# A two-layer hybrid diffusion step on one core: a longer ring for modulation weights, attention output formed token by feature, and a new order of the gated-linear-attention pass

## The chip, the cores and the metric

One core of a Trainium2 chip (trn2) runs the whole program. The metric is device time in microseconds (us), the median of the runs; lower is better. Engines are named as in the profile: PE (TensorE: matmuls, and PEld for its weight loads), DVE (VectorE), ACT (ScalarE), POOL (GpSimd), SP (SyncE, which issues most of the DMAs here).

## The reference, cut to what matters

```python
def adaln_layer(x, cond, mod_w, mod_b, norm_g, w1, w2, mixer):
    sh1, sc1, gt1, sh2, sc2, gt2 = modulation(cond, mod_w, mod_b)   # silu(cond) @ mod_w + mod_b
    h = rms_norm(x, norm_g[0]) * (1 + sc1) + sh1
    mix, aux = mixer(h)
    x = x + gt1 * rms_norm(mix, norm_g[1])
    ...
# layer 0 mixer: z = h @ w_in (2304 columns), then a gated convolution beside windowed attention
    s_loc = einsum(q, k of the own 128-token block and both neighbours) * scale, masked to +-128
    s_ctx = einsum(q, 256 cached context keys) * scale
    p = sink_softmax(concatenate([s_loc, s_ctx], -1), sink_f)   # 8 query heads, 2 key/value heads, 64 wide
    o = p[own] @ v_own + p[ctx] @ v_ctx
    return concatenate([conv_out, o], -1) @ w_out
# layer 1 mixer: bidirectional gated linear attention (GLA), 4 heads of 128 x 256, forward and backward
```

1152 tokens (128 prompt, 1024 latent) of 1024 features are 9 tiles of 128 tokens. All is float32. Products with the big weight matrices run as three float32r products of a high and a low part (hi x hi, hi x lo, lo x hi); attention and GLA use plain float32 products, each of which the trace shows as two loads and two matmuls.

## The kernel before, in words

Every engine has one program, written out by hand, with semaphores between them; nothing is scheduled by a compiler. An engine runs its list in order and stops at a wait. Three stages matter here.

**First pass** (54 units). A unit `u` is one 128-column panel of `ab_w_in` times 384 tokens: 24 matmuls of 384 columns into bank `u % 4` (`unit`). ACT empties the bank (`unit_take`). Between units the remaining 80 chunks of the modulation matrix are worked off. A chunk `k` is 512 KB: SP loads it into `mod_p[k % MODS]` once PE has used chunk `k - MODS` (`late_mod` on SP), ACT rounds it into `mod_ph` (`late_hi`), DVE subtracts to get the low part in place, `mod_pl` (`late_lo`), and PE multiplies both with the condition (`late_mod` on PE, 4 matmuls of 512 columns). Each four chunks finish one group of rows `q`: ACT copies the 4 x 512 sums out of PSUM (`late_rows`), PE turns them with four small transposes (`late_turn`, recorded at line 1687, the line of the helper `turn`), DVE adds them (`late_add`). Which chunks belong to a unit is `mods_after`, and which groups `rows_after`. In the list of ACT the rounding for unit `u + 1` stands behind `unit_take(u)`, and `late_rows` behind that rounding. From unit 18 on (`CONV_UNIT`) DVE also works out the convolution (`conv`), and in units 8 to 20 the rotary embedding (`rope`).

**Attention** (72 steps, `attention_steps`). A step is one block `b` of 128 queries and one head. Two steps (`u` = 0 and 1, heads `j` and `j + 4`) are a pair, 36 pairs in all. Block 0 has 1 tile of 128 keys, blocks 1 and 8 have 4, blocks 2 to 7 have 5 (24 pairs). The loop is staggered: in iteration `it` PE forms the scores of step `it` (line 1838), turns the probabilities of step `it - 2` (line 1687) and multiplies those of step `it - 3` with v (line 1864). DVE adds the band mask (1383), takes the maximum (1386, 1388), and for the step before divides the probabilities by their sum (1370, 1371, 1373). ACT takes the exponential (832, 835) and copies the turned probabilities of step `it - 3` to `prT` (822), three tiles; DVE copies the others (1359). The product with v has v as the stationary operand (64 columns) and 128 columns of `prT` as the moving one, so that the two heads of a pair come out feature by token, one above the other, in bank 2; ACT and DVE split that into `at_hi` (827) and `at_lo` (1364).

**GLA, backward pass** (9 tiles, `TURNS`). For each tile there are seven levels of decayed products. POOL forms gaps of the decay sums (lines 628 to 639), ACT takes their exponentials into PSUM (`exp_factor`, 1077 to 1085), DVE scales q and k (`scale`, 1581), PE multiplies (`gram`, 2099), DVE puts the result under a mask into `att` (`place`, 1591). Between levels stand, for the tile before, the update of the state (`update` on PE, 2086, and `state_step` on DVE, 1603) and its output (`att_out` on PE, 16 matmuls of 256 columns, 2116 and 2118; `o_take` on ACT, 1101), and a turn of k (`turn_k`).

Of the kernel before, what the change touches and what calls it, by code (L numbers as in the profile page):

```python
# [25 lines left out]
P = 128  # L26
# [17 lines left out]
GH = 4  # L44
# [7 lines left out]
MODS = 3  # L52
# [38 lines left out]
def build(nc, io):  # L91
# [17 lines left out]
    mod_p = [at(f"mod_p{i}", [P, 2, 512], F32, RW + 6 * PANEL + 2 * PANEL * i) for i in range(MODS)]  # L109
    mod_pl = [at(f"mod_pl{i}", [P, 2, 512], F32R, RW + 6 * PANEL + 2 * PANEL * i) for i in range(MODS)]  # L110
    mod_ph = [at(f"mod_ph{i}", [P, 2, 512], F32R, RW + 7 * PANEL + 2 * PANEL * i) for i in range(MODS)]
# [32 lines left out]
    smx = at("smx", [P, 3, 8], F32, o + 34816)  # L144
# [82 lines left out]
    with ExitStack() as ctx:  # L227
# [67 lines left out]
        s_norm = sem("s_norm")  # L295
        pt_ready = sem("pt_ready")
        pt_a = sem("pt_a")
        pt_v = sem("pt_v")
# [59 lines left out]
        O_BANK = 2  # L358
# [6 lines left out]

        def mods_after(u):
# [297 lines left out]
        def _(act):  # L664
# [150 lines left out]
            for it in range(len(steps) + 4):  # L815
                if 3 <= it < len(steps) + 3:
                    b, j, u, tiles = steps[it - 3]
# [6 lines left out]
                if it >= 4 and steps[it - 4][2] == 1:  # L824
                    b, j, u, tiles = steps[it - 4]
                    act.wait_ge(pv_ready, it - 3)
                    nc.scalar.activation(at_hi[:, b, j, :], ps[:, O_BANK, 0:P], ACT.Copy).then_inc(ao_hi, 1)
                if it < len(steps):
                    b, j, u, tiles = steps[it]
                    x = smx[:, it % 3, :]  # L830
                    act.wait_ge(s_max, it + 1)
                    nc.scalar.activation(prob[it % 3][:, 0:len(tiles) * P], s_bank(it)[:, 0:len(tiles) * P], ACT.Exp,  # L832
                                         bias=x[:, 1:2], accum_out=x[:, 2:3])
                    head = j + 4 * u
                    nc.scalar.activation(x[:, 3:4], sink[:, head:head + 1], ACT.Exp, bias=x[:, 1:2]).then_inc(s_exp, 1)
# [267 lines left out]
            for a, tile in enumerate(TURNS):  # L1103
                if tile != 1:
                    exp_factor("k1", tile)
                for level in range(NL):
                    if LEVELS[level] > 1:
                        exp_factor("S", tile, level)
                    if level == 0:
# [5 lines left out]
                    exp_factor("M", tile, level)  # L1115
# [5 lines left out]
                    if level == 4 and a:  # L1121
# [63 lines left out]
        def _(dve):  # L1185
# [85 lines left out]
            def late_lo(k):  # L1271

                dve.wait_ge(mod_hi, FIRST_LO + k + 1)
                V.tensor_tensor(mod_pl[k % MODS][:], mod_p[k % MODS][:], mod_ph[k % MODS][:].bitcast(F32),  # L1274
# [75 lines left out]
            wide = 0  # L1350
            for it in range(len(steps) + 4):
                if 3 <= it < len(steps) + 3:
                    b, j, u, tiles = steps[it - 3]
                    if len(tiles) > 3:
                        dve.wait_ge(pt_ready, it - 2)
                        if it >= 5:
                            dve.wait_ge(pv_ready, it - 4)
                        m = len(tiles) - 3
                        V.tensor_copy(prT[(it - 3) % 2][:, 3:3 + m, :],
                                      ps[:, 1, 0:m * P].rearrange("p (t n) -> p t n", t=m)).then_inc(pt_v, 1)  # L1360
                if it >= 4 and steps[it - 4][2] == 1:
                    b, j, u, tiles = steps[it - 4]
                    dve.wait_ge(ao_hi, (it - 4) // 2 + 1)
                    V.tensor_tensor(at_lo[:, b, j, :], ps[:, O_BANK, 0:P], at_hi[:, b, j, :].bitcast(F32),
                                    ALU.subtract).then_inc(ao_lo, 1)
                if 1 <= it <= len(steps):
                    b, j, u, tiles = steps[it - 1]
                    x = smx[:, (it - 1) % 3, :]
                    dve.wait_ge(s_exp, it)
                    own(V.tensor_tensor(x[:, 4:5], x[:, 2:3], x[:, 3:4], ALU.add))  # L1370
                    own(V.reciprocal(x[:, 5:6], x[:, 4:5]))
                    pr = prob[(it - 1) % 3][:, 0:len(tiles) * P]
                    V.tensor_scalar(pr, pr, x[:, 5:6], None, ALU.mult).then_inc(s_norm, 1)  # L1373
                if it < len(steps):
                    b, j, u, tiles = steps[it]
                    x = smx[:, it % 3, :]
# [9 lines left out]
                    own(V.tensor_reduce(x[:, 0:1], s[:, 0:len(tiles) * P], AX_X, ALU.max))  # L1386
# [850 lines left out]
```

## Time and profile before

| | before |
|---|---|
| median of 3 runs | 3229.49 us (3227.47 to 3234.83) |
| profiled execution, its time | 3222.65 us |
| span of its instructions | 3220.9 us |
| PE busy (matmul) | 2972.4 us, 92% |
| DVE busy | 1636.6 us, 51% |
| ACT busy | 1340.6 us, 42% |
| POOL busy | 159.7 us, 5% |

The three stages above lie at about 65 to 462, 463 to 731 and 2009 to 2222 us of the span. The rest is the opening, the output projections, two MLPs, the GLA projection and the forward pass; PE is busy there nearly all the time.

### The profile page before, as it was taken

The numbers are of one execution on the slowest core, as the hardware profiler recorded it, in microseconds if no ns is written. First come the engines' busy times: TensorE is split into PE (matmuls) and PEld (weight loads), VectorE is DVE, ScalarE is ACT, GpSimd is POOL, SyncE is SP. The second block draws the span as 40 slices with busy tenths as digits, with TensorE's granted clock in tenths as the row PEclk, the third lists the DMA queues.
The fourth block names the chain that finished last, engine by engine and source line by source line (L and its number), as shares of the span: only waits on it lengthen the run. The fifth ranks groups of instructions, "written<-read, shape, count | busy, mean of one in ns | idle before, by whom it ended". The sixth has DMA issues, their size and how long they took to land.

```text
span 3220.9 us, 39879 instructions
## 1 busy us (share of the span) xinstructions
PE 2972.4 (92%) x14994; PEld 2575.5 (80%) x14994; DVE 1636.6 (51%) x2527; ACT 1340.6 (42%) x2151; POOL 159.7 (5%) x260
## 2 busy tenths in 40 slices
PE   6888888888999999999999999777799999999998
PEld 3667676667899999999989877666679999999997
DVE  6444546664645454454442254766554545445444
ACT  6333333334544344344332366554444344334333
POOL 0000000000000000000000000873000000000000
PEclk8989989999999999999999999878899999999999
DMA  5444420005334443443331343001434444444443
GB/s 218 131 136 143 140 85 1 1 1 150 111 119 124 124 147 121 130 144 125 124 106 46 107 136 124 13 1 60 151 110 124 125 124 144 127 127 144 128 126 111
DMA packets 309592, 355.15 MB, mean 110 GB/s; under 512 B 20070, under 2 KB 242604, under 8 KB 308428
## 3 DMA queue, kind: packets, MB, share of 16 engines
q1 hardware_dynamic: 300560, 331.52, 32.9%
q10 hardware_dynamic: 6876, 13.87, 1.2%
q0 software_dynamic: 2016, 7.86, 0.7%
q8 instruction: 91, 1.49, 0.2%
q14 instruction: 49, 0.40, 0.0%
HBM read 337.88 MB, written 15.34 MB: 110 GB/s over the span
## 4 chain that ended last, share of the span: by engine, by line
PE 78%; DVE 9%; ACT 6%; issue 4%; DMA 3%; ACTq 0%; DVEq 0%; SPq 0%
PE ps L1897 35%; PE ps L1956 24%; PE ps L1746 7%; PE ps L2012 4%; PE ps L2099 2%; DMA mod_p<-mod_w 2%; PE ps L1687 2%; DVE smx L1386 1%; PE ps L1764 1%; DVE prob L1373 1%; DVE t_g L1409 1%; ACT junk_n L848 1%; DVE ps L1383 1%; PE ps L2116 1%; ACT mod_ph L726 0%
## 5 line engine op out<-in xcount | busy, mean ns | idle before, releaser
L1213 DVE TENSOR_TENSOR p_lo<-p_raw,p_hi 128x1024 fp32r<-128x1024 f32 x507 | 619.6, 1224 | 682.8 <-ACT p_hi L708 682.6
L708 ACT ACTIVATE p_hi<-p_raw 128x1024 fp32r<-128x1024 f32 x507 | 532.8, 1052 | 543.0 <-DMA p_raw<-mlp_w 398.7
L1956 PE MATMUL ps<-hm_hi,p_hi 128*128 128x384 f32 x1536 | 517.3, 337 | 4.8 <-DVE hm_lo L1233 4.0
L1956 PE MATMUL ps<-hm_hi,p_lo 128*128 128x384 f32 x1536 | 517.1, 337 | 0.0
L1956 PE MATMUL ps<-hm_lo,p_hi 128*128 128x384 f32 x1536 | 516.0, 336 | 0.0
L1897 PE MATMUL ps<-p_hi,hid_hi 128*128 128x512 f32 x1152 | 362.6, 396 | 1.9 <-DVE p_lo L1213 1.9
L1897 PE MATMUL ps<-p_lo,hid_hi 128*128 128x512 f32 x1152 | 357.3, 391 | 0.0
L1897 PE MATMUL ps<-p_hi,hid_lo 128*128 128x512 f32 x1152 | 356.5, 391 | 0.0
L893 ACT ACTIVATE relu<-ps 128x384 f32<-128x384 f32 x192 | 94.4, 492 | 547.9 <-PE ps L1956 547.9
L1447 DVE TENSOR_TENSOR sqr<-relu 128x384 f32<-128x384 f32 x192 | 107.2, 558 | 396.3 <-ACT relu L893 396.3
L1956 PEld LDWEIGHTS ps<-hm_hi,p_hi 128*128 128x128 f32 x1536 | 289.4, 188 | 14.1 <-DVE hm_lo L1233 4.5
L1956 PEld LDWEIGHTS ps<-hm_lo,p_hi 128*128 128x128 f32 x1536 | 289.5, 188 | 7.2
L1956 PEld LDWEIGHTS ps<-hm_hi,p_lo 128*128 128x128 f32 x1536 | 289.4, 188 | 0.0
L1897 PEld LDWEIGHTS ps<-p_lo,hid_hi 128*128 128x128 f32 x1152 | 216.3, 188 | 48.1
L1897 PEld LDWEIGHTS ps<-p_hi,hid_lo 128*128 128x128 f32 x1152 | 216.2, 188 | 47.6
L1897 PEld LDWEIGHTS ps<-p_hi,hid_hi 128*128 128x128 f32 x1152 | 210.3, 188 | 34.3 <-DVE p_lo L1213 2.4
L1274 DVE TENSOR_TENSOR mod_pl<-mod_p,mod_ph 128x1024 fp32r<-128x1024 f32 x80 | 96.9, 1224 | 180.5 <-ACT mod_ph L726 180.4
L1746 PE MATMUL ps<-h_hi,p_hi 128*128 128x384 f32 x432 | 159.5, 369 | 0.0
L1746 PE MATMUL ps<-h_lo,p_hi 128*128 128x384 f32 x432 | 151.3, 350 | 0.0
L1746 PE MATMUL ps<-h_hi,p_lo 128*128 128x384 f32 x432 | 151.2, 350 | 0.0
L2099 PE MATMUL ps<-xx,xx 128*128 128x128 f32 x432 | 76.1, 342 | 56.0 <-DVE xx L1581 34.5
L832 ACT ACTIVATE prob<-ps,smx 128x640 f32<-128x640 f32 (+2 forms) x72 | 52.0, 722 | 160.4 <-DVE smx L1388 160.4
(238 smaller groups left out, 4344.4 us busy)
## 6 DMA issues: line engine op xcount, KB each, us to landing
p_raw<-mlp_w SPq DMA_DIRECT2D x384, 512.0 KB, 3.8
mod_p<-mod_w SPq DMA_DIRECT2D x80, 512.0 KB, 4.1
p_raw<-gla_w_in SPq DMA_DIRECT2D x56, 512.0 KB, 3.6
p_raw<-gla_w_out SPq DMA_DIRECT2D x24, 512.0 KB, 3.4
mod_w<-mod_w SPq DMA_DIRECT2D x8, 1024.0 KB, 13.4
p_raw<-ab_w_in SPq DMA_DIRECT2D x14, 512.0 KB, 5.5
p_raw<-ab_w_out SPq DMA_DIRECT2D x12, 512.0 KB, 3.5
p_raw<-ab_w_out SPq DMA_DIRECT2D x24, 256.0 KB, 3.8
```

The lines of the kernel that those rows point to most:

```text
L708: nc.scalar.activation(p_hi[s][:, :, 0:width], p_raw[s][:, :, 0:width], ACT.Copy).then_inc(pan_hi, 1)
L832: nc.scalar.activation(prob[it % 3][:, 0:len(tiles) * P], s_bank(it)[:, 0:len(tiles) * P], ACT.Exp, bias=x[:, 1:2], accum_out=x[:, 2:3])
L893: nc.scalar.activation(relu[b][:], ps[:, b, 0:GN], ACT.Relu).then_inc(up_read[b], 1)
L1213: V.tensor_tensor(p_lo[s][:, :, 0:width], p_raw[s][:, :, 0:width], p_hi[s][:, :, 0:width].bitcast(F32), ALU.subtract).then_inc(pan_lo, 1)
L1274: V.tensor_tensor(mod_pl[k % MODS][:], mod_p[k % MODS][:], mod_ph[k % MODS][:].bitcast(F32), ALU.subtract).then_inc(mod_lo, 1)
L1447: V.tensor_tensor(sqr[b][:], relu[b][:], relu[b][:], ALU.mult).then_inc(sq_ready, 1)
L1687: return M.transpose(out, in_, ident[0:n, 0:n])
L1746: mm = M.matmul(ps[:, b, 0:GN], w[s][:, c, :], h0[n][x][:, c, :], start=(c == 0 and x == 0 and w is p_hi), stop=(c == DC - 1 and w is p_lo))
L1897: mm = M.matmul(acc(t)[:, cols], x, flat(w[s])[:, cols], start=begin and edge == 0, stop=end and edge == 2)
L1956: mm = M.matmul(ps[:, b, 0:GN], w[s][:, c, :], x[:, c, :], start=(c == 0 and x is hi and w is p_hi), stop=(c == DC - 1 and w is p_lo))
L2012: mm = M.matmul(ps[0:width, b, 0:GN], w[s][:, c, 0:width], hx[g][x][:, c, :], start=(c == 0 and x == 0 and w is p_hi), stop=(c == DC - 1 a ...
L2099: last = M.matmul(ps[:, i % 2, h * P:(h + 1) * P], stationary[:, h, :], moving[:, h, :], start=True, stop=True)
```

## The change

1. First pass: `MODS` goes from 3 to 4 raw buffers, and the rounded parts get a ring of their own of `MOD_HI` = 2 (the same six panels of memory). Chunks are given out two to a unit from unit 2 on, fewer in some units of the convolution. `late_rows` goes ahead of `unit_take` in ACT's list.
2. Attention: the probabilities are turned unscaled. The product with v now has the turned probabilities as the stationary operand (128 columns) and 64 columns of v as the moving one, so that the output stands token by feature, both heads of a pair side by side. DVE scales it with the reciprocal sums when it takes it from PSUM (two instructions of 64 columns, into `at_n`), PE turns it once for both heads into bank 7 (`AT_BANK`), and from there it is split. ACT alone copies `prT`, now 640 columns. Sum and reciprocal are formed once a pair.
3. GLA, backward: ACT's exponential for `M` goes ahead of the copy to `att` at level 0; `att_out` goes in two halves, behind the products of levels 2 and 3; `o_take` and `state_step` move from level 4 to 5, `turn_k` from level 5 to 6.

```diff
-MODS = 3
+MODS = 4
+MOD_HI = 2
...
+        mod_unit = []
+        for u in range(2, 49):
+            conv_u0 = u - CONV_UNIT
+            few = conv_u0 >= 0 and conv_u0 % 9 in (0, 4, 7)
+            mod_unit += [] if conv_u0 % 9 == 7 and few else [u] if few else [u, u]
+        mod_unit = mod_unit[:LATE]
...
-            return [k for k in range(LATE) if 2 + 46 * k // LATE == u]
+            return [k for k in range(LATE) if mod_unit[k] == u]
...
-            return [q for q in range(LATE // 4) if 2 + 46 * (4 * q + 3) // LATE + 1 == u]
+            return [q for q in range(LATE // 4) if mod_unit[4 * q + 3] + 1 == u]
...
-                if k >= MODS:
-                    act.wait_ge(modp_used, FIRST_USED + k - MODS + 1)
-                nc.scalar.activation(mod_ph[k % MODS][:], mod_p[k % MODS][:], ACT.Copy).then_inc(mod_hi, 1)
+                if k >= MOD_HI:
+                    act.wait_ge(modp_used, FIRST_USED + k - MOD_HI + 1)
+                nc.scalar.activation(mod_ph[k % MOD_HI][:], mod_p[k % MODS][:], ACT.Copy).then_inc(mod_hi, 1)
...
+                for q in rows_after(u):
+                    late_rows(q)
                 unit_take(u)
                 for k in mods_after(u + 1):
                     late_hi(k)
-                for q in rows_after(u):
-                    late_rows(q)
...
-                    m = min(3, len(tiles))
-                    nc.scalar.activation(prT[(it - 3) % 2][:, 0:m, :], ps[:, 0, 0:m * P].rearrange("p (t n) -> p t n", t=m),
+                    nc.scalar.activation(prT[(it - 3) % 2][:].rearrange("p t n -> p (t n)")[:, 0:n], psf[:, 0:n],
                                          ACT.Copy).then_inc(pt_a, 1)
...
+                if it >= 7 and it % 2:
+                    b, j, u, tiles = steps[it - 7]
+                    act.wait_ge(at_turned, (it - 7) // 2 + 1)
+                    nc.scalar.activation(at_hi[:, b, j, :], ps[:, AT_BANK, 0:P], ACT.Copy).then_inc(ao_hi, 1)
...
-                    V.tensor_scalar(pr, pr, x[:, 5:6], None, ALU.mult).then_inc(s_norm, 1)
...
+                    dve.wait_ge(pv_ready, 2 * pair + 2)
+                    if pair >= 2:
+                        dve.wait_ge(at_turned, pair - 1)
+                    for u in range(2):
+                        last = V.tensor_scalar(at_n[pair % 2][:, u, :], ps[:, O_BANK, HD * u:HD * (u + 1)], r[:, u:u + 1], None,
+                                               ALU.mult)
+                    last.then_inc(at_norm, 1)
...
+                if it >= 8 and it % 2 == 0:
+                    b, j, u, tiles = steps[it - 8]
+                    dve.wait_ge(ao_hi, (it - 8) // 2 + 1)
+                    V.tensor_tensor(at_lo[:, b, j, :], ps[:, AT_BANK, 0:P], at_hi[:, b, j, :].bitcast(F32),
+                                    ALU.subtract).then_inc(ao_lo, 1)
...
-                    pe.wait_ge(s_norm, it - 1)
+                    pe.wait_ge(s_exp, it - 1)
...
+                if it >= 6 and it % 2 == 0:
+                    pair = (it - 6) // 2
+                    pe.wait_ge(at_norm, pair + 1)
+                    if pair:
+                        pe.wait_ge(ao_lo, pair)
+                    turn(ps[:, AT_BANK, 0:P], at_n[pair % 2][:].rearrange("p u d -> p (u d)")).then_inc(at_turned, 1)
...
-                        last = M.matmul(ps[cols, O_BANK, 0:P], v, prT[(it - 3) % 2][:, pos, :],
+                        last = M.matmul(ps[:, O_BANK, cols], prT[(it - 3) % 2][:, pos, :], v,
                                         start=(pos == 0), stop=(pos == len(tiles) - 1))
...
+                    exp_factor("M", tile, level)
                     if level == 0:
...
-                    exp_factor("M", tile, level)
...
-                    if level == 4 and a:
+                    if level == 5 and a:
                         o_take(a - 1)
...
-                    if level == 4 and a:
+                    if level == 5 and a:
                         dve.wait_ge(ob_ready, a)
...
                     if level == 1 and a:
                         update(a - 1, TURNS[a - 1])
-                        att_out(a - 1)
-                    if level == 5 and tile != 1:
+                    if level in (2, 3) and a:
+                        att_out(a - 1, 2 * (level - 2), 2 * (level - 1))
+                    if level == 6 and tile != 1:
```

How the instructions stand on an engine, at three places. ACT in the first pass, units 13 and 14 of the kernel before (`mod_r` is the copy of `late_rows`, `q_t` that of `unit_take`, `mod_ph` that of `late_hi`):

```order
L744 ACTIVATE q_t<-ps 128x384 [waits unit_done3]
L726 ACTIVATE mod_ph_77<-mod_p_71 128x1024 [waits modp_used,modp_landed0]
L726 ACTIVATE mod_ph_78<-mod_p_72 128x1024 [waits modp_used,modp_landed1]
L733 ACTIVATE mod_r<-ps 4x512 [waits mod_turned,modp_used]
L708 ACTIVATE p_hi_171<-p_raw_163 128x1024 [waits pan_in2]
```

and of the changed kernel:

```order
L743 ACTIVATE mod_r<-ps 4x512 [waits mod_turned,modp_used]
L754 ACTIVATE q_t<-ps 128x384 [waits unit_done2]
L736 ACTIVATE mod_ph_79<-mod_p_73 128x1024 [waits modp_used,modp_landed2]
L736 ACTIVATE mod_ph_80<-mod_p_74 128x1024 [waits modp_used,modp_landed3]
L754 ACTIVATE q_t<-ps 128x384 [waits unit_done3]
```

The copy of the sums stood behind two roundings, each of which waits for a landing; it now stands ahead of the unit's own copy and of the roundings that belong to it.

DVE in the attention of blocks 2 to 7, one pair, before:

```order
L1383 TENSOR_TENSOR ps<-ps,band 128x128 [waits s_ready]
L1386 TENSOR_REDUCE smx<-ps 128x1 [waits dve_own]
L1388 TENSOR_SCALAR smx<-smx,sink 128x1 [waits dve_own]
L1359 COPY prT_106<-ps 128x256 [waits pv_ready,pt_ready]
L1364 TENSOR_TENSOR at_lo<-ps,at_hi 128x128 [waits ao_hi]
L1370 TENSOR_TENSOR smx<-smx 128x1 [waits s_exp]
L1371 RECIPROCAL smx<-smx 128x1 [waits dve_own]
L1373 TENSOR_SCALAR prob_104<-prob_104,smx 128x640 [waits dve_own]
```

and now (first an odd iteration, then an even one):

```order
L1368 TENSOR_SCALAR at_n_110<-ps,smx 128x64 [waits at_turned,pv_ready]
L1380 TENSOR_TENSOR ps<-ps,band 128x128 [waits s_ready]
L1383 TENSOR_REDUCE smx<-ps 128x1 [waits dve_own]
L1385 TENSOR_SCALAR smx<-smx,sink 128x1 [waits dve_own]
L1390 TENSOR_TENSOR smx<-smx 128x2 [waits s_exp]
L1391 RECIPROCAL smx<-smx 128x2 [waits dve_own]
L1380 TENSOR_TENSOR ps<-ps,band 128x128 [waits s_ready,dve_own]
L1395 TENSOR_TENSOR at_lo<-ps,at_hi 128x128 [waits ao_hi]
```

The 640-column scaling and the copy to `prT` are gone from DVE; `at_lo` stands behind the maximum of its iteration.

PE in the same stage, the even iteration of the changed kernel, in which the output of a pair is turned:

```order
L1844 MATMUL ps<-kc_t,q_t 128x256 [waits s_exp]
L1844 MATMUL ps<-k_t,q_t 128x256
L1844 MATMUL ps<-k_t,q_t 128x128
L1694 MATMUL ps<-ident,prob_106 128x128 [waits pt_a,s_exp]
L1694 MATMUL ps<-ident,at_n_110 128x128 [waits ao_lo,at_norm]
L1869 MATMUL ps<-v_c,prT_108 128x64 [waits pt_a]
```

The turn of `at_n` waits for `ao_lo`, the count of `at_lo`, which DVE raises in the same even iteration, behind the maximum of the scores that head this list.

## Rows read from the trace of the kernel before

**Rows 1.** Windows: busy us and instructions of each engine, TensorE clock, DMA share, GB/s.

```profile
core 0: us, PE busy (x) PEld busy (x) DVE busy (x) ACT busy (x) POOL busy (x), PEclk, DMA share, GB/s
82.00:461.50 379.50, 328.27 (x1656) 266.24 (x1654) 174.57 (x230) 127.48 (x172) 0.00 (x0) 0.94 0.42 132
479.20:507.90 28.70, 27.82 (x106) 18.20 (x105) 16.71 (x58) 10.54 (x36) 0.00 (x0) 0.65 0.00 1
507.90:698.40 190.50, 159.77 (x1001) 129.57 (x1000) 131.62 (x409) 73.34 (x216) 0.00 (x0) 0.97 0.00 1
2010.00:2222.00 212.00, 155.10 (x812) 142.82 (x810) 145.44 (x241) 106.72 (x178) 152.08 (x245) 0.79 0.03 10
```

**Rows 2.** Waits, first pass (65 to 462 us): us in total, times, longest.

```profile
ACT mod_ph L726 <- DMA mod_p<-mod_w: 74.4, 25, 3.6
PE ps L1687 <- ACT mod_r L733: 42.0, 14, 4.7
PE ps L1687 <- ACT v_n L799: 4.7, 1, 4.7
```

**Rows 3.** The chain that ended last, first pass: start, us, what.

```profile
93.88 1.07 ACT mod_ph L726
94.97 1.24 DVE mod_pl L1274
...
297.96 1.85 PE ps L1764 x8
...
440.52 21.04 PE ps L1746 x120
```

**Rows 4.** DMA issues of the stage: count, KB each, median us to landing.

```profile
mod_p<-mod_w SPq DMA_DIRECT2D x71, 512.0 KB, 4.0
```

**Rows 5.** Timeline, one `late_turn`, weight loads: start, us, engine, instruction.

```profile
97.27 0.32 PEld L1687 LDWEIGHTS ps<-ident,mod_r 4*128 4x128 f32 x4 [0.47 <-ACT mod_r L733]
```

**Rows 6.** Timeline, attention, one pair of five-tile steps.

```profile
602.27 0.49 DVE L1383 TENSOR_TENSOR ps<-ps,band 128x128 f32<-128x128 f32 x2
...
603.01 0.70 PE L1838 MATMUL ps<-kc_t,q_t 64*128 64x256 f32 x2
...
603.54 0.81 PE L1838 MATMUL ps<-k_t,q_t 64*128 64x256 f32 x4
603.65 0.22 DVE L1388 TENSOR_SCALAR smx<-smx,sink 128x1 f32<-128x1 f32 x1
603.78 0.41 DVE L1359 COPY prT<-ps 128x256 f32<-128x256 f32 x1
603.90 0.79 ACT L832 ACTIVATE prob<-ps,smx 128x640 f32<-128x640 f32 x1 [2.73 <-DVE smx L1388]
...
604.87 0.48 ACT L822 ACTIVATE prT<-ps 128x384 f32<-128x384 f32 x1
...
609.04 0.74 PE L1687 MATMUL ps<-ident,prob 128*128 128x128 f32 x5 [0.34 <-issue]
609.14 0.29 DVE L1364 TENSOR_TENSOR at_lo<-ps,at_hi 128x128 fp32r<-128x128 f32 x1 [1.35 <-ACT at_hi L827]
...
609.71 0.41 PEld L1864 LDWEIGHTS ps<-prT,v_c 128*64 128x64 f32 x4 [0.17 <-issue]
...
610.94 0.29 PEld L1838 LDWEIGHTS ps<-kc_t,q_t 64*128 64x128 f32 x2 [0.17 <-issue]
```

**Rows 7.** Timeline, attention, block 1: scores and turn of four tiles, no wait between.

```profile
499.07 0.74 PE L1838 MATMUL ps<-kc_t,q_t 64*128 64x256 f32 x2
...
500.18 0.66 PE L1687 MATMUL ps<-ident,prob 128*128 128x128 f32 x4
```

**Rows 8.** Timeline, GLA, one tile of the backward pass.

```profile
2108.43 1.95 PE L2099 MATMUL ps<-xx,xx 128*128 128x128 f32 x16
...
2109.53 0.74 DVE L1591 COPY_PREDICATED att<-masks,ps 128x512 f32<-128x512 int32 x1 [2.88 <-PE ps L2099]
...
2122.23 0.69 DVE L1581 TENSOR_TENSOR xx<-gq,ps 128x512 f32<-128x512 f32 x1 [1.81 <-ACT ps L1085]
```

More of the change, by code:

```diff
@@ L108, in build @@
     mod_r4 = at("mod_r4", [4, 2 * D], F32, RS + 1024)
-    mod_p = [at(f"mod_p{i}", [P, 2, 512], F32, RW + 6 * PANEL + 2 * PANEL * i) for i in range(MODS)]
-    mod_pl = [at(f"mod_pl{i}", [P, 2, 512], F32R, RW + 6 * PANEL + 2 * PANEL * i) for i in range(MODS)]
-    mod_ph = [at(f"mod_ph{i}", [P, 2, 512], F32R, RW + 7 * PANEL + 2 * PANEL * i) for i in range(MODS)]
+    mod_p = [at(f"mod_p{i}", [P, 2, 512], F32, RW + (6 + i) * PANEL) for i in range(MODS)]
+    mod_pl = [at(f"mod_pl{i}", [P, 2, 512], F32R, RW + (6 + i) * PANEL) for i in range(MODS)]
+    mod_ph = [at(f"mod_ph{i}", [P, 2, 512], F32R, RW + (6 + MODS + i) * PANEL) for i in range(MOD_HI)]
     def acts(name, dt, r, chunks=DC):
@@ L143, in build @@
     prT = [at(f"prT{i}", [P, 5, P], F32, o + 29696 + 2560 * i) for i in range(2)]
-    smx = at("smx", [P, 3, 8], F32, o + 34816)
+    smx = at("smx", [P, 3, 4, 2], F32, o + 34816)
+    at_n = [at(f"at_n{i}", [P, 2, HD], F32, o + 34944 + 512 * i) for i in range(2)]
     gq = at("gq", [P, TILES, GH, P], F32, RD)
@@ L814, in _ @@
             steps = attention_steps()
-            for it in range(len(steps) + 4):
+            for it in range(len(steps) + 7):
                 if 3 <= it < len(steps) + 3:
-                    b, j, u, tiles = steps[it - 3]
+                    n = len(steps[it - 3][3]) * P
                     act.wait_ge(pt_ready, it - 2)
@@ L1349, in _ @@
             steps = attention_steps()
[L1350 to L1372, printed above, removed]
-                    V.tensor_scalar(pr, pr, x[:, 5:6], None, ALU.mult).then_inc(s_norm, 1)
+            for it in range(len(steps) + 8):
+                pair = (it - 5) // 2
+                if it >= 5 and it % 2 and pair < len(steps) // 2:
+                    r = smx[:, pair % 3, 0]
+                    dve.wait_ge(pv_ready, 2 * pair + 2)
[5 more added lines that the diff above has]
+                    last.then_inc(at_norm, 1)
                 if it < len(steps):
                     b, j, u, tiles = steps[it]
-                    x = smx[:, it % 3, :]
+                    x = smx[:, it // 2 % 3]
                     s = s_bank(it)
@@ L1385, in _ @@
                         own(last)
-                    own(V.tensor_reduce(x[:, 0:1], s[:, 0:len(tiles) * P], AX_X, ALU.max))
+                    own(V.tensor_reduce(x[:, 0, u:u + 1], s[:, 0:len(tiles) * P], AX_X, ALU.max))
                     head = j + 4 * u
-                    V.tensor_scalar(x[:, 1:2], x[:, 0:1], sink[:, head:head + 1], -1.0, ALU.max, ALU.mult).then_inc(s_max, 1)
+                    V.tensor_scalar(x[:, 1, u:u + 1], x[:, 0, u:u + 1], sink[:, head:head + 1], -1.0, ALU.max,
+                                    ALU.mult).then_inc(s_max, 1)
+                if it >= 3 and it % 2 and it - 2 < len(steps):
+                    x = smx[:, (it - 3) // 2 % 3]
+                    dve.wait_ge(s_exp, it - 1)
+                    own(V.tensor_tensor(x[:, 2], x[:, 2], x[:, 3], ALU.add))
+                    own(V.reciprocal(x[:, 0], x[:, 2]))
+                if it >= 8 and it % 2 == 0:
[3 more added lines that the diff above has]
+                                    ALU.subtract).then_inc(ao_lo, 1)
             dve.wait_ge(mods_ready, 2)
@@ L1761, in late_mod @@
                 pe.wait_ge(mod_lo, FIRST_LO + k + 1)
-                for w in (mod_ph[k % MODS], mod_pl[k % MODS]):
+                for w in (mod_ph[k % MOD_HI], mod_pl[k % MODS]):
                     for a in range(2):
                         last = M.matmul(ps[0:4, 4 + q % 2, :], csr[:, 2 * (k % 4) + a, :], w[:, a, :],
-                                        start=(k % 4 == 0 and a == 0 and w is mod_ph[k % MODS]),
+                                        start=(k % 4 == 0 and a == 0 and w is mod_ph[k % MOD_HI]),
                                         stop=(k % 4 == 3 and a == 1 and w is mod_pl[k % MODS]))
@@ L1820, in _ @@
             steps = attention_steps()
-            wide = [i for i, st_ in enumerate(steps) if len(st_[3]) > 3]
-            for it in range(len(steps) + 3):
+            for it in range(len(steps) + 5):
                 if it < len(steps):
@@ L2100, in gram, with att_out @@
                 last.then_inc(gram_ready, 1)
-            def att_out(a):
+            def att_out(a, h0, h1):
                 tile = TURNS[a]
-                pe.wait_ge(gram_taken, NL * (a + 1))
-                if a:
-                    pe.wait_ge(ob_taken, a)
-                    pe.wait_ge(xt_ready, factor_at[("q1", tile, 0)] + 1)
-                pe.wait_ge(khn_ready, min(a + 1, TILES - 1))
-                if a == 1:
-                    pe.wait_ge(st_in, 16)
-                if a >= 2:
-                    pe.wait_ge(st_ready, a)
-                for h in range(GH):
+                if h0 == 0:
+                    pe.wait_ge(gram_taken, NL * (a + 1))
+                    if a:
+                        pe.wait_ge(ob_taken, a)
+                        pe.wait_ge(xt_ready, factor_at[("q1", tile, 0)] + 1)
+                    pe.wait_ge(khn_ready, min(a + 1, TILES - 1))
+                    if a == 1:
+                        pe.wait_ge(st_in, 16)
+                    if a >= 2:
+                        pe.wait_ge(st_ready, a)
+                for h in range(h0, h1):
                     o = psf[:, 3 * 512 + DV * h:3 * 512 + DV * (h + 1)]
@@ L2134, in _ @@
                         turn_k(kh, 3)
-            att_out(TILES - 1)
+            att_out(TILES - 1, 0, GH)
             def turn_k0(tile):
```

36 lines of the change are left out of this document (14 added, 22 removed).

## The prediction

> **What bounds the kernel now.** I read the windows first, for how full PE is in the three stages that change, then in each stage the waits and the timeline, because the stages have different limits.
>
> In the first pass PE is busy 328.3 of 379.5 us and its granted clock is 0.94 on the mean [rows 1]. So 51.2 us are idle, and up to 0.06 x 379.5 = 22.8 us are lost to stretches at the lower of its two levels (1.2 against 2.4 GHz). The reader is to see in the waits where the idle time lies: 42.0 us of it stand before the four small transposes of `late_turn`, which wait for ACT's copy `mod_r` [rows 2]. ACT itself is not full (127 of 379.5 us [rows 1]). It stands for 74.4 us before the rounding of chunks that have not landed [rows 2], and the copy is queued behind these roundings. Ring and order together make the wait; no engine is the bound.
>
> In the attention of blocks 2 to 7 (190.5 us for 24 pairs, 7.94 us each) PE is busy 84% and DVE 69% [rows 1], and neither is full. One step runs through DVE (mask, maximum), ACT (exponential), DVE (sum, reciprocal, scaling) before DVE may begin the next mask, so the two take turns. The timeline shows ACT idle 2.73 us for the maximum, and DVE idle 1.35 us for `at_hi` [rows 6].
>
> In the backward pass of GLA (212 us for 9 tiles, 23.6 each) the clock is down to 0.79, and PE 73%, DVE 69%, POOL 72% are all half waiting [rows 1]. Twice per tile DVE stands for something that only the order puts ahead: 2.88 us for a product that is behind the 16 matmuls of `att_out`, and 1.81 us for an exponential that is behind ACT's copy to `att` [rows 8].
>
> **The change, part by part.**
>
> *First pass.* The work is the same: 54 units, 80 chunks. A unit takes PE 21.04 / 5 = 4.21 us, a chunk 1.85 / 2 = 0.93 [rows 3], so a unit with two chunks lasts 6.06 us. A buffer freed by chunk k of one unit is needed again for rounding behind the unit copy of the next, at least 0.93 + 4.21 = 5.1 us later; a landing takes 4.0 [rows 4]. The load is two chunks a unit and a panel in three units, 3.5 MB in 18.2 us or 192 GB/s; now 132 GB/s take a DMA share of 0.42 [rows 1], so that would take 0.61. Two roundings and two subtractions (1.07 and 1.24 each [rows 3]) behind a unit's end are done about 0.5 + 0.93 + 2.1 + 1.24 = 4.8 us later, ahead of the 6.06 at which PE wants them; the second ring of two holds them. That is the cover: with landings of 6 us or more it is gone, and `late_hi` waits again. The copy `mod_r` now needs only what PE did a unit ago, so the 42.0 us go. I leave 8 us of idle time: the wait for `v_n` (4.7 [rows 2], its place is unchanged and now meets two roundings) and about 1 us at each of three places where the long convolution on DVE comes ahead of a subtraction. Of the clock loss I count back 16 of 22.8, since full PE stretches (the five units of [rows 3]) run at the higher level. Saved: 51.2 - 8 + 16 = 59 us. Bounds: 74 (all), and 25 if the wait only moves to the landing.
>
> *Attention.* DVE loses the scaling, the copy and half the sums; it no longer waits for the exponential of the step before. ACT's copy grows from 384 to 640 columns (0.48 us to about 0.7); its 0.97 us from exponential to copy stays [rows 6], so 1.7 us a step, far from full. What comes last now? PE's list. An even iteration begins with the scores: issued at 0, drained at 0.53 + 0.81 = 1.34. DVE then needs 1.51 from the first mask to the instruction behind the maximum, and 0.29 for `at_lo` [rows 6]. With 0.03 and 0.10 from engine to engine (0.03 is seen from maximum to exponential, 0.10 is my estimate), the turn of `at_n`, which waits for this `at_lo`, starts at 3.27. Scores and turn of the five tiles would be through at 1.35 + 0.67 = 2.02 (1.11 in [rows 7] for four tiles, and 2 x 0.122 for the fifth; 609.04 to 609.71 in [rows 6]). So a new wait of 1.25 us per pair takes the place of DVE's. Behind it on PE stand the product with v and the next scores, and all of DVE and ACT follows these. Turn and switch are 0.22 (one fifth of 0.67, and some 0.09). If V is the product with v, an even iteration is 3.49 + V, an odd one 2.02 + V, a pair 5.51 + 2V.
>
> V is the unknown. Now 64 stationary and 128 moving columns take 1.23 us (609.71 to 610.94, of which 0.17 is issue [rows 6]). Afterwards it is 128 stationary and 64 moving. No row has this. The nearest is the GLA product with 128 of both: 16 in 1.95, 0.122 each [rows 8]. That is more than the 1.06 / 10 = 0.106 with 64 stationary columns, so there the load sets the pace, and halving what moves should not help. Below: 4 loads of 128 columns for transposes, with 4 moving, take 0.32 [rows 5], 0.08 each at most, but those are one pass, not two. V is 10 x 0.122 + 0.15 = 1.37 by the first, 0.95 by the second. I take the first: same kind of instruction. A pair is then 8.25, 0.31 more than now, x 24 = +7 us. Pairs of four tiles wait in the same way; block 1 runs mostly at the lower clock (0.65 [rows 1]), where PE's part counts double: +3. The longer tail (scaling, turn, split): +1. Together +11; from V = 0.95: 24 x -0.53 = -13, with the other two terms -9.
>
> The Trainium skill, on the page TensorE: Matmul & The Clock Gate, section LDWEIGHTS (loading the stationary operand), speaks against this edit: the time of a weight load goes with the columns of the stationary operand, not with its depth, and the change doubles them. By its figure, 128 / 1.2 = 107 ns, V would be 1.22 and a pair 7.95, attention +4 and the kernel 3148. The trace does not have the figure: its one-pass load is at most 80 ns, its two-pass spacing 122.
>
> *GLA.* If both order waits vanish, 2.88 + 1.81 = 4.7 us a tile. The product of level 2 is no longer behind 16 matmuls, and half of `att_out` falls into PE's waits. Given back: `turn_k` behind the last level makes DVE's next `kh` wait, about 0.6; POOL, busy 152.1 / 9 = 16.9 us a tile [rows 1], becomes nearly full at 19, which costs some 0.7. I take 3.4 x 8 tiles (the first has no tile before it) = 27. Bounds: 0, if another wait ends at the same time, and (23.6 - 16.9) x 8 = 54, where POOL is the bound.
>
> **Sum:** -59 + 11 - 27 = -75. The profiled execution took 3222.65, so 3147.7; the median of the runs is 6.8 above it, so 3154.5, given as 3155.
>
> **The rivals.**
> 1. *The product with v follows its moving columns*: 0.061 each, V = 0.76, pair 7.03, -22, with the rest about -22: 3229.5 - 59 - 27 - 25 = 3118. For it: PE hides loads behind matmuls elsewhere. Against it: 0.122 with 128 stationary columns [rows 8]. 0.14.
> 2. *The ring is still short*: landings at 192 GB/s take over 6 us and PE waits for `mod_pl` in place of `mod_r`. First pass -25: 3189. The share of 0.61 speaks against it, a panel ahead in the queue for it. 0.12.
> 3. *The GLA order does not do what it says*: POOL or the low clock (0.79) keeps the period, 0 in place of -27: 3182. 0.10.
> 4. *Slower*: the granted clock. In attention PE now waits 1.25 us in one piece each pair. If it ran blocks 2 to 7 at the lower level, the even iteration is 2.44 + 0.03 + 1.80 + 0.10 + 0.35 + 2.6 = 7.3, the odd 2.45 + 1.3 + 2.6 = 6.35, a pair 13.7, so +138: 3229.5 - 86 + 142 = 3285. It decides from 86 / 5.8 = 15 of 24 pairs on. Against it: the clock is 0.97 today with waits as long [rows 1, 6]; for it: 0.65 in block 1. 0.04.
>
> **How the numbers follow.** Forecast 0.60, the rivals 0.14, 0.12, 0.10, 0.04. The likeliest gives 3155; its own range is 3132 to 3178 (first pass 45 to 68, GLA 15 to 38, attention 0 to 20, not all at one end). The range for 8 in 10 reaches into rivals 1, 2 and 3: 3122 to 3188. A measurement of this kernel tells 0.2% (6.5 us) from no change. Faster 0.94 (all but rival 4 and mixtures), same 0.02, slower 0.04.
>
> **What would show it.** First pass: the waits have no `mod_r` of tens of us, DMA waits of ACT fall below 20 us, the stage (first chunk's product to last unit) lasts about 320 us at a clock near 0.98. Attention: a row of PE waiting for DVE `at_lo` before a line 1694 transpose, about 36 x 1.2 = 43 us; a pair lasts 8.1 to 8.4 us; ten loads of `prT` take 1.2 us. GLA: a tile lasts near 20 us, and PE's gap before the level 2 product is gone. The prediction fails if V is below 1 us, if PE's waits for `mod_pl` reach 20 us, or if the clock rows of attention fall below 0.9.

## The result, and the profile after

The changed kernel takes 3266.55 us (median of 4 runs, 3265.22 to 3271.31) against 3229.52 us of the kernel before (4 runs on the same chip). Its ratio to before is 1.0115, with a 95% interval of 1.0097 to 1.0132. It is 37 us slower; I had forecast 75 us faster, and the time lies far outside the range. It lies 18 us below the 3285 us of the slower rival.

Three stages changed, and they went different ways. The page of the changed kernel, span and granted clock in 40 slices of 81.6 us each:

```profile
span 3265.5 us, 39825 instructions
PE   5999999999999999999999999877799999999998
PEclk8999955555999999999999999988999999999999
```

The five slices with a 5 are the attention. The reader should see that the row above them does not fall with them: PE is listed as busy while its clock is granted at the lower of its two levels, 1.2 GHz. The windows of the changed kernel say the same with numbers:

```profile
core 0: us, PE busy (x) PEld busy (x) DVE busy (x) ACT busy (x) POOL busy (x), PEclk, DMA share, GB/s
82.00:395.20 313.20, 307.89 (x1656) 250.06 (x1655) 171.90 (x230) 129.02 (x172) 0.00 (x0) 1.00 0.50 158
397.00:409.30 12.30, 9.16 (x34) 6.75 (x34) 6.29 (x34) 6.86 (x30) 0.00 (x0) 0.63 0.30 97
409.30:440.00 30.70, 27.33 (x85) 19.40 (x85) 11.48 (x38) 9.68 (x32) 0.00 (x0) 0.50 0.00 1
440.00:760.00 320.00, 299.92 (x1084) 253.55 (x1085) 100.80 (x330) 88.63 (x233) 0.00 (x0) 0.50 0.00 1
803.00:850.00 47.00, 41.87 (x178) 33.49 (x179) 20.18 (x20) 20.16 (x30) 0.00 (x0) 0.93 0.60 190
...
2080.00:2241.00 161.00, 121.99 (x720) 110.90 (x720) 130.12 (x214) 94.66 (x161) 141.63 (x230) 0.87 0.04 15
```

**First pass.** The stretch that took 379.5 us [rows 1] takes 313.2, with 5.3 us idle and the upper level throughout: 66.3 us saved.

**Attention.** The exponentials of the 72 steps show its length, first to last start, for the kernel before and then for the changed one:

```profile
L832 ACT ACTIVATE prob<-ps,smx x72: 367/793/794, 465.7 to 727.3; 128x640 f32<-128x640 f32 x48, 128x512 f32<-128x512 f32 x16, 128x128 f32<-128x128 f32 x8
```

```profile
L841 ACT ACTIVATE prob<-ps,smx x72: 354/793/795, 399.3 to 791.5; 128x640 f32<-128x640 f32 x48, 128x512 f32<-128x512 f32 x16, 128x128 f32<-128x128 f32 x8
```

That is 392.2 us instead of 261.6, 130.6 more. With its end (the last output is turned and split; the last `at_lo` is done at 733.4 us before and at 802.3 now) it is 403.0 instead of 267.7, 135.3 more. The lower level begins in block 0 and stays for the whole stage. The timeline of one pair of five-tile steps, PE, from the even step's scores (597.15) to those of the next pair (609.83):

```profile
597.15 1.22 PE L1844 MATMUL ps<-kc_t,q_t 64*128 64x256 f32 x2
598.17 1.49 PE L1844 MATMUL ps<-k_t,q_t 64*128 64x256 f32 x4
...
601.71 0.45 PE L1694 MATMUL ps<-ident,at_n 128*128 128x128 f32 x1 [0.80 <-DVE at_lo L1395]
...
604.11 1.22 PE L1844 MATMUL ps<-kc_t,q_t 64*128 64x256 f32 x2
...
606.54 1.33 PE L1694 MATMUL ps<-ident,prob 128*128 128x128 f32 x5
607.67 0.96 PE L1869 MATMUL ps<-v_c,prT 128*128 128x64 f32 x4
608.42 1.49 PE L1869 MATMUL ps<-v_n,prT 128*128 128x64 f32 x6
609.83 1.22 PE L1844 MATMUL ps<-kc_t,q_t 64*128 64x256 f32 x2
```

A pair takes 12.68 us (6.96 even, 5.72 odd) in place of 7.94. The two score rows that headed a pair before, 0.70 and 0.81 [rows 6], are 1.22 and 1.49 now, and the product with v takes 609.83 - 607.67 = 2.16. The waits of the stage (397 to 803 us) have the row that I had forecast, PE for `at_lo`; I had put it at 43 us, and it is 26.4:

```profile
ACT prob L841 <- DVE smx L1385: 279.9, 70, 5.1
DVE ps L1380 <- PE ps L1844: 175.4, 64, 3.9
DVE at_n L1368 <- PE ps L1869: 86.8, 35, 4.0
...
PE ps L1694 <- DVE at_lo L1395: 26.4, 33, 1.3
```

DVE waits for PE and ACT for DVE, while PE is idle for 31 of the 406 us. PE is the bound of this stage now.

**GLA, backward.** From the first to the last product of level 0 it is 158.9 us (2080.8 to 2239.7) instead of 183.2: 24.3 saved. DVE's wait ahead of `att` fell from 31.9 to 10.9 us:

```profile
DVE att L1598 <- PE ps L2104: 10.9, 17, 1.2
```

The sum of the stages is -66.3 - 24.3 + 135.3 = +44.7, and the spans differ by 3265.5 - 3220.9 = 44.6 (the medians by 37; the profiled execution of before, 3222.65 us, lies 6.9 below its median). So the whole result is in three known places. Two gained about what they should. What has to be explained is why the clock stayed down.

### The profile page after: what moved, and what is told of

The parts are those of the page before. It is cut to its first block and busy times, and to the rows that moved or that the text cites. A ratio compares the mean times of both kernels' runs of the same rounds, so it can differ in the third digit from the quotient of the medians.

```text
span 3265.5 us, 39825 instructions
## 1 busy us (share of the span) xinstructions
PE 3087.6 (95%) x15030; PEld 2680.1 (82%) x15030; DVE 1587.0 (49%) x2391; ACT 1352.7 (41%) x2151; POOL 159.2 (5%) x260
## 3 DMA queue, kind: packets, MB, share of 16 engines
q8 instruction: 91, 1.49, 0.2%
## 5 line engine op out<-in xcount | busy, mean ns | idle before, releaser
L1753 PE MATMUL ps<-h_hi,p_hi 128*128 128x384 f32 x432 | 151.8, 351 | 0.0
L1457 DVE TENSOR_TENSOR hid_lo<-sqr,hid_hi 128x384 fp32r<-128x384 f32 x192 | 107.3, 559 | 18.5 <-DVE sqr L1454 0.4
```

Of the source, the lines that this page charges most:

```text
L1457: V.tensor_tensor(hid[layer][b][1][:], sqr[b][:], hid[layer][b][0][:].bitcast(F32), ALU.subtract).then_inc(hid_lo, 1)
L1753: mm = M.matmul(ps[:, b, 0:GN], w[s][:, c, :], h0[n][x][:, c, :], start=(c == 0 and x == 0 and w is p_hi), stop=(c == DC - 1 and w is p_lo))
```

## The experiments

The theories, before the runs. A: the product with v in its new form (a load of 128 columns ahead of each 64 moving ones) keeps the clock low, however busy PE is listed. B: PE's wait for `at_lo`, once a pair, keeps it low. C: the level depends on how block 0 is entered, and stays from there. D: the fuller first pass ahead of it is needed. C was put up after the first four runs of the stage (`e1_old_attention`, `e2_attention_alone`, `e3_both_heads_of_v`, `e5_lo_first`), the others before them. The table lists the experiments in their order below; "exponentials" is the time from the first to the last start of the 72. The kernel before, run on the same chips, gave 3228.57 us (beside e1, e2, e3 and e5), 3230.24 (e4, e6, e7, e8) and 3228.09 (e9, e10). Where a row has one run, it has no interval; the other kernels' runs spread over 3 to 19 us, so of these rows only differences well above that, or readings of the stage itself, are used.

| run | us (runs) | ratio to before | clock of the span | exponentials, us |
|---|---|---|---|---|
| e1_old_attention | 3131.7 (4) | 0.9698 (0.9681 to 0.9714) | 0.975 | 260.1 |
| e2_attention_alone | 3363.78 (1) | | 0.91 | 392.2 |
| e3_both_heads_of_v | 3150.2 (4) | 0.9771 (0.9741 to 0.9801) | 0.972 | 271.2 |
| e5_lo_first | 3240.89 (1) | | 0.923 | 358.7 |
| e4_filled_block0 | 3272.04 (1) | | 0.925 | 389.8 |
| e8_filled_lo_first | 3245.22 (1) | | 0.927 | 366.9 |
| e6_wide_lo_first | 3097.43 (4) | 0.9593 (0.9577 to 0.9609) | 0.976 | 219.3 |
| e7_rows_behind | 3180.21 (1) | | 0.969 | 261.9 |
| e9_ring_of_three | 3154.3 (4) | 0.9771 (0.9755 to 0.9787) | 0.971 | 261.8 |
| e10_gla_before | 3156.19 (4) | 0.9783 (0.9766 to 0.9799) | 0.972 | 260.4 |

### The attention of before in the changed kernel, and the new attention alone

`e1_old_attention` takes the three attention loops, their semaphores and tiles from the kernel before and leaves the first pass and GLA changed. `e2_attention_alone` is the reverse.

```diff
-    smx = at("smx", [P, 3, 4, 2], F32, o + 34816)
-    at_n = [at(f"at_n{i}", [P, 2, HD], F32, o + 34944 + 512 * i) for i in range(2)]
+    smx = at("smx", [P, 3, 8], F32, o + 34816)
...
-                        last = M.matmul(ps[:, O_BANK, cols], prT[(it - 3) % 2][:, pos, :], v,
+                        last = M.matmul(ps[cols, O_BANK, 0:P], v, prT[(it - 3) % 2][:, pos, :],
```

> The changed kernel with the attention of the kernel before; first pass and GLA stay as changed. Theory A (the low clock comes with the new attention itself): the granted clock recovers some 34 us into attention as before, attention takes 268 to 272 us, the kernel about 3229.5 - 66.5 - 24.4 = 3139 us. Rival D (it comes from the fuller first pass ahead of it): the clock stays at the lower level here too, attention takes well over 320 us, and the kernel is above 3190.

> The kernel before with the new attention alone. Theory A: the clock stays at the lower level for the whole of attention as in the changed kernel, which costs 135 us: about 3356 to 3360 us. Rival D (the fuller first pass is needed for it): the clock recovers, attention takes 270 to 285 us, the kernel 3230 to 3245.

Without the new attention the other two parts give 3131.7 us, 97 less than before; with it alone the kernel is 135 us slower (one run). Both met theory A; they came out 7 us below the 3139 and 4 above the 3360 that it gave. The window of `e1_old_attention` in which the changed kernel has 0.50:

```profile
440.00:600.00 160.00, 132.22 (x842) 107.03 (x841) 110.90 (x345) 61.27 (x181) 0.00 (x0) 0.99 0.00 1
```

PE is busy for 83% of it at the upper level. In `e2_attention_alone` the exponentials take 392.2 us, to the tenth what they take in the changed kernel, behind the first pass of before. Its clock is down there too:

```profile
480.00:800.00 320.00, 297.86 (x1061) 248.28 (x1061) 102.62 (x336) 89.66 (x241) 0.00 (x0) 0.50 0.00 1
```

D falls: the attention makes its own clock.

### Both heads of v as the moving operand

Only the moving operand of the product with v is widened from one head's 64 columns to all 128. The half that belongs to the other head is worked out and not read. Everything else, the wait for `at_lo` too, stays.

```diff
-                        v = v_c[:, tile, cols] if what == "ctx" else v_n[:, tile, cols]
-                        last = M.matmul(ps[:, O_BANK, cols], prT[(it - 3) % 2][:, pos, :], v,
+                        v = v_c[:, tile, :] if what == "ctx" else v_n[:, tile, :]
+                        last = M.matmul(ps[:, O_BANK, P * u:P * (u + 1)], prT[(it - 3) % 2][:, pos, :], v,
```

> The changed kernel, but the product with v moves all 128 columns of v (both key/value heads; the half that isn't wanted is left unread) past the same 128 stationary columns, so that loads, waits and order stay and only the moving columns of this product double. Theory A1 (the clock stays low because PE streams too little between loads): the clock recovers within some 34 us, a pair takes about 8.3 us, attention 275 to 285 us, the kernel 3140 to 3150. Rival B (it is PE's wait for at_lo in each pair) and rival D: no recovery, a pair takes 11.2 us or more, the kernel about 3267.

More work for PE makes the kernel 116 us faster than the changed one. Windows of this kernel:

```profile
409.30:440.00 30.70, 26.48 (x111) 18.80 (x110) 13.57 (x47) 11.15 (x37) 0.00 (x0) 0.71 0.00 1
440.00:600.00 160.00, 135.16 (x797) 114.86 (x798) 74.18 (x244) 65.71 (x171) 0.00 (x0) 0.90 0.00 1
```

PE is less busy (84%) than in the changed kernel (94%), and its clock is 0.90 instead of 0.50. The wait for `at_lo` is still there, so it alone does not hold the clock down. Its timeline also gives the terms of my sum at the upper level. Scores of the even step begin at 563.01, of the odd one at 567.76, of the next pair at 570.85:

```profile
563.01 0.70 PE L1844 MATMUL ps<-kc_t,q_t 64*128 64x256 f32 x2
...
564.75 0.74 PE L1694 MATMUL ps<-ident,prob 128*128 128x128 f32 x5 [0.39 <-ACT prT L831]
...
566.41 0.30 PE L1694 MATMUL ps<-ident,at_n 128*128 128x128 f32 x1 [0.93 <-DVE at_lo L1395]
...
566.55 0.61 PE L1869 MATMUL ps<-v_c,prT 128*128 128x128 f32 x4
...
567.00 0.83 PE L1869 MATMUL ps<-v_n,prT 128*128 128x128 f32 x6
...
567.76 0.70 PE L1844 MATMUL ps<-kc_t,q_t 64*128 64x256 f32 x2
```

The turn of `at_n` starts 3.40 us behind the scores, the product takes 567.76 - 566.55 = 1.21, and a pair 7.84.

### The split ahead of the maximum

In DVE's even iteration `at_lo` goes ahead of mask and maximum, so that PE finds it done.

```diff
+                if it >= 8 and it % 2 == 0:
+                    b, j, u, tiles = steps[it - 8]
+                    dve.wait_ge(ao_hi, (it - 8) // 2 + 1)
+                    V.tensor_tensor(at_lo[:, b, j, :], ps[:, AT_BANK, 0:P], at_hi[:, b, j, :].bitcast(F32),
+                                    ALU.subtract).then_inc(ao_lo, 1)
                 if it < len(steps):
                     b, j, u, tiles = steps[it]
...
-                if it >= 8 and it % 2 == 0:
-                    b, j, u, tiles = steps[it - 8]
...
```

> The changed kernel with at_lo ahead of the maximum in DVE's even iteration, so that PE's turn of the output finds it done; nothing else is changed. Rival B (the wait for at_lo keeps the clock low): the clock recovers and the kernel takes 3130 to 3140. Theory A1: the 26 us of waits go, the clock stays at the lower level, attention shortens by 25 to 30 us, the kernel about 3238.

The window of this kernel is the clearest row of the study:

```profile
440.00:700.00 260.00, 260.00 (x961) 227.96 (x960) 91.82 (x295) 77.92 (x202) 0.00 (x0) 0.50 0.00 1
```

PE is listed as busy for 260.00 of 260.00 us, and the clock is at the lower level for all of it. The wait is gone, but the clock is not back. B falls. The exponentials take 33.5 us less than in the changed kernel, 7 more than the 26.4 us of listed waits. The whole kernel gains only 25.7, because later stages give some of it back; the same GLA stretch takes 162.7 us here and 158.9 there. That the kernel's gain equals the listed waits is chance.

### Block 0 filled up

Four products of 256 columns into a bank that nobody reads are added to each of the first nine iterations, so that the clock is up when block 1 begins. `e8_filled_lo_first` has both this and the edit above.

```diff
+                if it < 9:
+                    for _ in range(4):
+                        M.matmul(ps[:, 6, 0:256], ident[:], q_t[:, 0, 0:256], start=True, stop=True)
```

> The changed kernel with four extra products of 256 columns per iteration on PE through the nine iterations 0 to 8 of attention (block 0), into a bank that nothing reads, so that PE is full there and the clock should not fall at its start. If the low state holds only because attention begins in it (theory C), the clock stays at its upper level in blocks 1 to 8, a pair takes about 8.0 to 8.3 us, attention about 275 to 290 us and the kernel 3140 to 3155. If the narrow product itself can't hold the level (rival A2), the clock falls in one of the first dips and stays down: attention between 330 and 410 us, the kernel 3200 to 3275.

> Block 0 filled as in the run of that name, and at_lo ahead of the maximum, with the narrow product of the changed kernel. Theory C: the clock stays up and a pair loses the wait of about 1 us, the kernel 3115 to 3130. Rival A2: the clock falls and stays down, 3190 to 3250, less than the changed kernel by 25 us for the waits.

The windows of `e4_filled_block0`, block 0 and the first pairs of block 1:

```profile
410.00:420.00 10.00, 10.00 (x50) 8.18 (x49) 3.65 (x17) 2.92 (x13) 0.00 (x0) 1.00 0.01 2
420.00:430.00 10.00, 8.42 (x48) 6.19 (x47) 6.06 (x22) 5.48 (x18) 0.00 (x0) 1.00 0.00 0
430.00:450.00 20.00, 17.25 (x79) 13.84 (x79) 7.89 (x26) 7.75 (x23) 0.00 (x0) 0.69 0.00 1
450.00:500.00 50.00, 46.80 (x171) 39.59 (x170) 15.91 (x52) 13.92 (x37) 0.00 (x0) 0.50 0.00 0
```

The stage is entered at the upper level, holds it while the filling products run (the last is issued at about 420 us) and for some 16 us behind them, then falls and stays down. With the wait gone too (`e8_filled_lo_first`) it also stays down, with 366.9 us of exponentials:

```profile
450.00:700.00 250.00, 250.00 (x922) 219.06 (x922) 87.58 (x279) 75.53 (x197) 0.00 (x0) 0.50 0.00 1
```

C falls, and A is left: with the narrow product, and without filling, the stage neither reached the upper level nor kept it. One thing stays open. While the filling products ran, the narrow product was in the same list (two matmuls a step in block 0) and the level was the upper one. So these runs do not tell whether the product with v has to be the wider one, or whether more moved columns anywhere in the list would do; no run adds them elsewhere in blocks 1 to 8. The one stretch at the upper level also prices the narrow product, here for four tiles:

```profile
427.33 0.56 PE L1872 MATMUL ps<-v_c,prT 128*128 128x64 f32 x4
427.72 0.61 PE L1872 MATMUL ps<-v_n,prT 128*128 128x64 f32 x4
428.26 0.48 PE L1844 MATMUL ps<-kc_t,q_t 64*128 64x256 f32 x1
```

428.26 - 427.33 = 0.93 for eight, 0.116 each. The wide one takes 1.21 / 10 = 0.121. Half the moving columns save almost nothing. What the two have alike is the load of 128 columns, so I read it as what sets the pace.

### The two edits that help, together

> The wide product with v (128 moving columns) and at_lo ahead of the maximum, both. The clock recovers as with the wide product alone, and the wait for at_lo, 0.93 us in a pair at the upper level, goes: 30 us by the row of waits less what the next wait takes (ACT's copy of prT). Expected 3118 to 3132 us, below the kernel with the old attention (3131.7). If ACT's exponential and copy take the whole place of it, 3145 to 3150.

Its windows, and a pair of its timeline (517.92 to 524.65, 6.73 us):

```profile
409.30:440.00 30.70, 29.64 (x140) 22.61 (x140) 16.95 (x55) 13.99 (x45) 0.00 (x0) 0.77 0.00 1
440.00:600.00 160.00, 150.83 (x1023) 132.30 (x1022) 96.64 (x310) 83.55 (x216) 0.00 (x0) 1.00 0.00 1
```

```profile
517.92 0.70 PE L1844 MATMUL ps<-kc_t,q_t 64*128 64x256 f32 x2
...
521.01 0.70 PE L1844 MATMUL ps<-kc_t,q_t 64*128 64x256 f32 x2
...
523.33 0.27 PE L1694 MATMUL ps<-ident,at_n 128*128 128x128 f32 x1
...
524.65 0.70 PE L1844 MATMUL ps<-kc_t,q_t 64*128 64x256 f32 x2
```

3097.43 us is the best version: 4.1% below the kernel before, and 21 us below the lower end of what I expected (3118). Its exponentials take 219.3 us against 261.6 in the kernel before, so the new form of attention gains 42 us once the clock is back. The same edit of DVE's order shortens the exponentials by 51.9 us at the wide product and by 33.5 at the narrow one. At the wide one more than PE's wait went: that was 29.8 us in 33 times; and the clock, 0.90 with the wait, is 1.00 without it. So the wait does cost clock, at the wide product.

### The parts of the first pass, and the order of GLA

All three stand on `e1_old_attention`. `e7_rows_behind` puts `late_rows` back behind the roundings (the first diff); `e9_ring_of_three` keeps the new order and has three raw and three rounded buffers (the second); `e10_gla_before` has GLA's lists of before.

```diff
-                for q in rows_after(u):
-                    late_rows(q)
                 unit_take(u)
                 for k in mods_after(u + 1):
                     late_hi(k)
+                for q in rows_after(u):
+                    late_rows(q)
```

```diff
-MODS = 4
-MOD_HI = 2
+MODS = 3
+MOD_HI = 3
```

> The kernel with the old attention and the changed first pass and GLA, but the copy of late_rows back behind the roundings in ACT's list; the ring of four and the schedule of chunks stay. If the place in the list made the wait (my reading), the copy comes some 3 us behind a unit's end and PE's waits for mod_r return, 25 to 40 us in total, the kernel 3157 to 3172. If it was the landing of chunks, which the longer ring hides (rival), the waits stay under 10 us, the kernel 3130 to 3141.

> The changed kernel with the attention of before, and in the first pass the new order and the new giving out of chunks, but three raw and three rounded buffers as before the change (MODS = 3, MOD_HI = 3). Theory R (the place of the copy in ACT's list made the wait, the ring did not): the copy's transposes do not wait, a buffer comes back one chunk earlier, and that is hidden by the landing of 4 us; 3132 to 3140 us, first pass within 5 us of 313, PE waits for mod_pl under 5 us. Theory S (the fourth raw buffer is needed, because two chunks to a unit ask for a landing in less than one unit): ACT waits for DMA again for tens of us, PE for mod_pl for 20 us or more; 3155 us or more.

> The changed kernel with the attention of before and the backward GLA pass in the order of before; alone the first pass is changed. Theory G (the GLA order is worth what its stage shows, 24 us): 3156 us, between 3151 and 3161, and the first pass at 313 us. Theory H (the stage gains by the clock or by what stands ahead of it, not by its order): within 5 us of 3132.

The first exponential of attention starts at 465.7 us in the kernel before, at 399.5 in `e1_old_attention`, 446.4 in `e7_rows_behind` and 418.4 in `e9_ring_of_three`. So undoing ACT's order costs 46.9 us (one run; the kernel, 3180.21 us, lies above the 3157 to 3172 that I expected) and undoing the ring 18.9, together 65.8 of the 66.2 that the whole part brings. Unless they interact, nothing is left for the new giving out of the chunks, which stands in both runs and was not tried alone. The waits of `e7_rows_behind` and then of `e9_ring_of_three`:

```profile
PEld ps L1696 <- ACT mod_r L742: 41.8, 19, 3.3
...
PE ps L1696 <- ACT mod_r L742: 32.3, 19, 2.9
```

```profile
DVE mod_pl L1283 <- ACT mod_ph L735: 142.0, 59, 7.8
ACT mod_ph L735 <- DMA mod_p<-mod_w: 86.8, 31, 3.7
```

With the copy behind the roundings PE's wait for `mod_r` is back, 32.3 us, though the ring is long; the clock is 0.95 from 82 to 440 us, where the stage had 0.99, which I estimate at most of the rest of the 46.9. With three buffers ACT waits for landings again (none are left with four), and PE loses 19 us; so it is the fourth raw buffer that takes the landing off the path. `e9_ring_of_three` came within 1 us of the 3155 of its second theory, but not by the wait that I had named: the weight loads wait 6.8 us for `mod_pl`, not 20. From 82 to 395.2 us PE is idle 17.6 us there and 5.3 in `e1_old_attention`, and the clock is 0.97 instead of 0.99, which by my estimate make up the 19 us together; 5.7 of the idle time are longer waits for `v_n` (8.8 us against 3.1).

`e10_gla_before` is 24.5 us behind `e1_old_attention` by the medians, 18.0 by the profiled spans, and its GLA stage is 178.4 us against 162.5, so 15.9 in the stage. The kernel before took 183.2 with the same order (clock 0.80 there, 0.81 here), and the changed one 158.9 with the other order (0.87, against 0.85 in `e1_old_attention`). So 4 to 5 us of such a difference come and go without a change of the order, and the order is worth 16 to 24 us.

## Why the prediction was wrong

- **First pass.** Forecast -59, measured -66.3, by the mechanism named: no wait for `mod_r` is left, none of ACT for a landing either. I had kept 8 us idle and 7 of clock loss; 5.3 us idle were left and the clock was 1.00.
- **The product with v.** I took 1.37 us for ten (0.122 each and 0.15). Wide, it takes 1.21; narrow at the upper level, 0.116 each. The reading that the load sets the pace fits both, and rival 1, that the time follows the moving columns, falls (its own sum was off too: its parts give -18 for attention, or 3125 us, where it took -25 and 3118). From the page TensorE: Matmul & The Clock Gate of the Trainium skill, section LDWEIGHTS (loading the stationary operand), the estimate was V = 1.22 (ten times 107 ns, and 0.15); the wide form meets that sum with 1.21, though its spacing is 0.121 and not 0.107 us.
- **The wait for at_lo.** Forecast at 3.27 us behind the scores and 1.25 long; it came at 3.40 at the upper level, 0.93 long there (scores and turn of the five tiles ended later than I had it) and 0.80 at the lower one. The whole pair, forecast at 8.25, is 7.84 in `e3_both_heads_of_v`. By its exponentials that kernel's attention is 9.6 us longer than before; my term was +11, but part of the 9.6 is its clock of 0.90.
- **GLA.** Forecast -27, measured -24.3 in the result, 19.9 us for a tile where I had said near 20; the order alone accounts for 16 to 24.
- **The step that failed** is the attention term of the sum: +11 forecast, +135.3 measured. For the 24 pairs of blocks 2 to 7 it took every time on PE at the upper level, on the ground given against the fourth rival, "Against it: the clock is 0.97 today with waits as long". I weighed the clock by idle time alone, and gave its loss 0.04. Of my signs of failure the last one came, clock rows of attention below 0.9. The runs show in its place that the stage ran at 0.50, and that the edit that decides is not the wait but the halved moving operand: `e5_lo_first` has no idle time and 0.50, `e3_both_heads_of_v` has 16% idle and 0.90. The rival's size was near: pair 13.7 forecast (7.3 and 6.35), 12.68 measured (6.96 and 5.72); attention +142 forecast, +135.3 measured. So the slow clock was written down, with a wrong cause and too small a chance, and with 2.6 for the product at the lower level where it takes 2.16.
- The clock of `e5_lo_first` is 0.50 with PE listed as busy for 260.00 of 260.00 us. The page TensorE: Matmul & The Clock Gate of the Trainium skill, section Part 1: The HAM clock gate, ties the lower level to idle stretches of PE and the upper one to sustained work. By that rule this stretch would run at the upper level, and the trace does not agree.

Shown are: that the new attention alone brings the loss, that 128 in place of 64 moving columns takes it away, and that taking away the wait, or entering the stage at the upper level, does not. What it is in the narrow product that keeps the level down, or whether wider work elsewhere in the list would lift it as well, no run takes apart.

## What to carry to other kernels

Where an edit swaps operands, compare how many columns move per load before and after, not only the time of the product: with 128 stationary and 64 moving columns it took as long here as with 128 moving, and the whole stage then ran at half the clock. Read the granted clock beside PE's busy share, since a PE that is listed as full may be full only because it is slow. And where one list holds a copy that another engine waits for behind work that waits for transfers, move the copy first: here the place in the list was worth 47 us and the fourth buffer 19.

## What was not expected of the hardware

- The granted clock stayed at 1.2 GHz for 409 us on end with PE busy 93% of the time, in the changed kernel (from 400 us on) and in `e2_attention_alone`, and through 260 us without a gap in `e5_lo_first`.
- Working out twice as many columns made the attention 121 us shorter (392.2 to 271.2 us of exponentials).
- From the upper level the stage did not fall at once: in `e4_filled_block0` the window of 420 to 430 us still has 1.00, the next 20 us 0.69, and then it is 0.50 to the end of the stage.
